# Where eight attention heads and a norm stand relative to a chunkwise delta rule, in one kernel of two transformer blocks

## The reference, cut to what matters

```
def token_mixer(h, rel_bias, w_in, conv_w, a_log, dt_bias, onorm_w, w_up_a, w_up_b, w_out):
    proj = h @ w_in
    qa, ka, va, qkv_b, z_b, b_b, a_b, gate_a, gate_b = jnp.split(proj, offs, axis=-1)
    y_a = moba_attention(heads_a(qa), heads_a(ka), heads_a(va), rel_bias)     # 8 heads of 64
    qkv_b = jax.nn.silu(causal_depthwise_conv(qkv_b, conv_w))
    q_b, k_b, v_b = (t.reshape(B, S, H_B, HD_B) for t in jnp.split(qkv_b, 3, axis=-1))
    beta = jax.nn.sigmoid(b_b)
    g = -jnp.exp(a_log) * jax.nn.softplus(a_b + dt_bias)
    o_b = gated_delta_rule(q_b, k_b, v_b, beta, g)                            # 4 heads of 128
    o_b = rms_norm(o_b, onorm_w) * jax.nn.silu(z_b.reshape(B, S, H_B, HD_B))
    y_b = o_b.reshape(B, S, W_B)
    m = jax.nn.sigmoid(gate_a) * (y_a @ w_up_a) + jax.nn.sigmoid(gate_b) * (y_b @ w_up_b)
    return m @ w_out
```

## Time and profile before

| | |
|---|---|
| runs of the kernel | 1547.35, 1551.43, 1552.74 us (median 1551.43) |
| profiled execution | 1547.66 us, span of the trace 1545.9 us |
| PE busy | 1447.2 us, 94% of the span |
| DVE, ACT busy | 763.5 us (49%), 619.6 us (40%) |
| mean granted TensorE clock | 0.949 |

### The profile page before, as it was taken

The page is one execution under the profiler, slowest core; times in us unless marked ns, Lnnn a source line. Parts: engine busy times, 40 slices in busy tenths (PEclk is TensorE's granted clock), DMA queues, the critical chain, the costliest instruction groups (busy, mean ns, idle before and its releaser), DMA issues.

```text
span 1545.9 us, 26177 instructions
## 1 busy us (share of the span) xinstructions
PE 1447.2 (94%) x10140; PEld 1233.4 (80%) x10140; DVE 763.5 (49%) x1280; ACT 619.6 (40%) x1022; POOL 10.5 (1%) x23
## 2 busy tenths in 40 slices
PE   5999999999999998899999989899878899999996
PEld 4899999899997995589999889799747856555553
DVE  4466654656545663356665456865157432221223
ACT  4445553543334552344444356533143322232222
POOL 0000020000000000000000000000000000000000
PEclk8999999999999998799999989999659899999998
DMA  7664455655556443466555454433003249999992
GB/s 311 127 187 137 137 164 177 222 174 177 177 174 218 155 150 110 145 213 221 185 190 182 160 178 150 139 108 98 26 0 123 96 184 373 366 355 371 371 367 96
DMA packets 80139, 289.65 MB, mean 187 GB/s; under 512 B 9520, under 2 KB 10544, under 8 KB 79920
## 3 DMA queue, kind: packets, MB, share of 16 engines
q1 hardware_dynamic: 77760, 280.00, 51.8%
q0 software_dynamic: 1712, 3.68, 1.6%
q10 hardware_dynamic: 576, 4.65, 0.7%
HBM read 285.14 MB, written 3.15 MB: 186 GB/s over the span
## 4 chain that ended last, share of the span: by engine, by line
PE 83%; DVE 9%; ACT 3%; DMA 2%; issue 2%; SPq 0%; ACTq 0%; DVEq 0%
PE bank L652 17%; PE bank L656 16%; PE bank L655 16%; PE bank L1184 11%; PE bank L1152 4%; DMA ring<-weights 2%; PE bank L716 2%; PE bank L793 2%; PE bank L687 1%; ACT w_hi L1255 1%; PE bank L1174 1%; PE bank L1175 1%; DVE ring_low L1641 1%; DVE hn L1656 1%; DVE sq L1976 1%
## 5 line engine op out<-in xcount | busy, mean ns | idle before, releaser
L1641 DVE TENSOR_TENSOR ring_low<-ring,w_hi 128x1024 fp32r<-128x1024 f32 x292 | 356.0, 1224 | 318.0 <-ACT w_hi L1255 315.5
L652 PE MATMUL bank<-hn_hi,w_hi 128*128 128x272 f32 (+1 forms) x1456 | 425.2, 292 | 24.2 <-DVE ring_low L1641 9.6
L656 PE MATMUL bank<-hn_hi,ring_low 128*128 128x272 f32 (+1 forms) x1456 | 418.5, 287 | 0.0
L655 PE MATMUL bank<-hn_low,w_hi 128*128 128x272 f32 (+1 forms) x1456 | 417.8, 287 | 0.0
L1255 ACT ACTIVATE w_hi<-ring 128x1024 fp32r<-128x1024 f32 x292 | 307.2, 1055 | 223.3 <-PE bank L652 181.5
L652 PEld LDWEIGHTS bank<-hn_hi,w_hi 128*128 128x128 f32 x1456 | 277.6, 191 | 31.2 <-issue 13.5
L656 PEld LDWEIGHTS bank<-hn_hi,ring_low 128*128 128x128 f32 x1456 | 278.1, 191 | 0.0
L655 PEld LDWEIGHTS bank<-hn_low,w_hi 128*128 128x128 f32 x1456 | 277.7, 191 | 0.2
L652 PE MATMUL bank<-arena_r,w_hi 128*128 128x256 f32 (+1 forms) x848 | 245.2, 289 | 12.0 <-DVE mod L1689 2.9
L656 PE MATMUL bank<-arena_r,ring_low 128*128 128x256 f32 (+1 forms) x848 | 242.8, 286 | 0.0
L655 PE MATMUL bank<-arena_r,w_hi 128*128 128x256 f32 (+1 forms) x848 | 242.3, 286 | 0.0
(11 more groups left out here) (333 smaller groups left out, 1431.5 us busy)
## 6 DMA issues: line engine op xcount, KB each, us to landing
ring<-weights SPq DMA_DIRECT2D x532, 512.0 KB, 4.4
tab<-tables ACTq DMA_DIRECT2D x1, 3129.0 KB, 12.8
skew<-arena POOLq DMA_DIRECT2D x1, 2048.0 KB, 46.4
h<-tokens ACTq DMA_DIRECT2D x2, 544.0 KB, 4.2
tab<-skew POOLq DMA_DIRECT2D x8, 128.0 KB, 3.8
out<-hn SPq DMA_DIRECT2D x8, 128.0 KB, 2.0
tab<-skew POOLq DMA_DIRECT2D x8, 64.0 KB, 3.6
vec<-vectors ACTq DMA_DIRECT2D x1, 321.5 KB, 5.1
```

The costliest lines, as they stand in the source:

```text
L652: begun = mm(dst[:, 0:cols], wh, high(k), start=k == 0, stop=False)
L655: mm(dst[:, 0:cols], wh, low(k), start=False, stop=False)
L656: last = mm(dst[:, 0:cols], wl, high(k), start=False, stop=k == K - 1)
L1641: tt_(ring_lo[:, slot, :], ring[:, slot, :], w_hi[:, n % SPLITS, :], ALU.subtract).then_inc(S("w_lo_ready"), 1)
```

## The change

Four edits, all in the second block's mixer; the mathematics is the same.

1. The attention loop is taken apart. Its scores, transposes and values get numbers among the rotating tiles (`turn`, `score`, `value`, banks 0 to 3), its buffers `p_a` and `pt_a` move into `sq`, `o_a_hi` and `o_a_lo` over and behind `q_a`. `moba(j)` on PE is: transposes of head j, scores of head j + 2, values of head j - 1. One call stands in each of nine places of the delta rule: after the gram product, after the turn of k, in levels 1 to 5 in place of the first gate tile, after `w`, and ahead of the scan. ACT and DVE get the matching pieces (`moba_exp`, `moba_turned`, `moba_store`; `moba_front`, `moba_probs`, `moba_low`).
2. The gate tiles that this displaces, and one more, move into the scan: tile 8 + 2c behind the product with the state, tile 9 + 2c behind the increment. Three of the four `z` tiles move to between gram, q by k and the turns.
3. The norms of q, k and `o_b`: the squares stand as the stationary side with one column of ones moving, so sums come out with tokens on partitions, 128 x 16 (128 x 8 for `o_b`). Root and reciprocal are taken there, and PE spreads the result back over rows by a product with the identity, two products for q and k and one for `o_b`; DVE multiplies from PSUM.
4. The weights of the two up projections are stored one after the other: all 8 half tiles of the attention (`upa`) first, with the norm of `o_b` between them, then the 8 of the delta rule (`upb`). DVE puts gate times `upa` into `m_up` and adds `upb` later.

Layout, tile order and the sums on PE:

```diff
-    out.append(narrow_units(np.concatenate([i["w_up_a_2"][0].reshape(512, DT, P), i["w_up_b_2"][0].reshape(512, DT, P)],
-                                           axis=0).reshape(D, D)))
+    out.append(narrow_units(i["w_up_a_2"][0]))
+    out.append(narrow_units(i["w_up_b_2"][0]))
...
-        tiles("z", BH, DT)
-        tiles("gates", 16, DT)
-        tiles("aa", AH, 0)
-        tiles("up", 2 * DT, 4)
...
+        z_tiles(0)
+        tiles(("score", 0), 1, 0)
+        tiles(("score", 1), 1, 0)
+        moba_tiles(0)
+        z_tiles(1)
+        z_tiles(2)
+        moba_tiles(1)
+        z_tiles(3)
+        gate_tiles(0, 2)
+        for lv in range(1, 6):
+            moba_tiles(lv + 1)
+            gate_tiles(lv + 1)
+        moba_tiles(AH - 1)
+        gate_tiles(7)
+        moba_tiles(AH)
+        gate_tiles(8, 8)
+        tiles("upa", DT, 4)
+        tiles("upb", DT, 4)
...
-            pe.wait_ge(S("exp_rows"), 1)
-            for j in range(4):
-                last = mm(bank[4 + j][:, :], ones, l2sq[:, j * 512:(j + 1) * 512], start=True, stop=True)
+            for p in range(2 * NP):
+                last = mm(bank[4][:, p:p + 1], l2sq[:, p * P:(p + 1) * P], ones[:, 0:1], start=True, stop=True)
             last.then_inc(S("l2_summed"), 1)
             wide(DT, hb, hb_lo, [(0, P), (P, SEQ)])
-            for t in range(BH):
+            pe.wait_ge(S("dec_diff"), 1)
+            pe.wait_ge(S("exp_rows"), 1)
+            pe.wait_ge(S("l2_inverted"), 1)
+            for p in range(NP, 2 * NP):
+                last = mm(bank[4 + p // 4][:, (p % 4) * P:(p % 4 + 1) * P],
+                          stats[:, 16 + p:17 + p].to_broadcast([P, P]), ident, start=True, stop=True)
+            last.then_inc(S("l2_rows"), 1)
```

The rest of PE's order:

```diff
+            def moba(j):
+
+                if j < AH:
+                    pe.wait_ge(S("moba_p"), j + 1)
+                    dst, pv = next_tile(("turn", j)), p_a[:, j % 2, :]
+                    nc.tensor.transpose(dst[:, 0:P], pv[:, 0:P], ident)
+                    nc.tensor.transpose(dst[:, P:2 * P], pv[:, P:2 * P], ident)
+                    nc.tensor.transpose(dst[:, 2 * P:3 * P], pv[:, 2 * P:3 * P], ident).then_inc(tile_done, 1)
+                if j + 2 < AH:
+                    moba_score(j + 2)
+                if j:
+                    v = j - 1
+                    if v == 0:
+                        wait_stored(pe, at["va"] + 1)
+                    dst, cols = next_tile(("value", v)), slice(v // 2 * P, (v // 2 + 1) * P)
+                    wait_stored(pe, at["turn", v])
+                    mm(dst[:, 0:SEQ], v_a[:, 0, cols], pt_a[:, v % 2, 0:SEQ], start=True, stop=False,
+                       skip_group_check=True)
+                    mm(dst[:, P:SEQ], v_a[:, 1, cols], pt_a[:, v % 2, SEQ:3 * P], start=False, stop=True,
+                       skip_group_check=True).then_inc(tile_done, 1)
+
+            hb_tile(("z", 0))
+            moba_score(0)
+            moba_score(1)
...
-            dense(DT, hb, hb_lo, SEQ)
+            moba(0)
+            hb_tile(("z", 1))
...
+            hb_tile(("z", 2))
...
+            moba(1)
+            hb_tile(("z", 3))
...
-            dense(DT, hb, hb_lo, SEQ)
-            dense(DT, hb, hb_lo, SEQ)
+            gate(0)
...
                 last.then_inc(S("mx_done"), 1)
-                dense(DT, hb, hb_lo, SEQ)
                 if lv == 0:
+                    gate(1)
                     continue
+                moba(lv + 1)
...
-                dense(DT, hb, hb_lo, SEQ)
+                gate(lv + 1)
...
-            dense(DT, hb, hb_lo, SEQ)
+            moba(AH - 1)
+            gate(7)
...
                 if c == 0:
+                    moba(AH)
...
+                gate(8 + 2 * c)
...
-            assert pos[1] == at["aa"]
-
+                gate(9 + 2 * c)
...
+            up_a()
             pe.wait_ge(S("ob_squared"), 1)
-            for j in range(2):
-                last = mm(bank[4 + j][:, :], ones, obsq[:, j * 512:(j + 1) * 512], start=True, stop=True)
+            for p in range(NP):
+                last = mm(bank[4][:, p:p + 1], obsq[:, p * P:(p + 1) * P], ones[:, 0:1], start=True, stop=True)
             last.then_inc(S("ob_summed"), 1)
...
+            up_a()
+            up_a()
+            pe.wait_ge(S("ob_inverted"), 1)
+            for p in range(NP):
+                last = mm(bank[6 + p // 4][:, (p % 4) * P:(p % 4 + 1) * P],
+                          stats[:, 8 + p:9 + p].to_broadcast([P, P]), ident, start=True, stop=True)
+            last.then_inc(S("ob_rows"), 1)
+            for t in range(3, DT):
+                up_a()
             for t in range(DT):
-                dense(4, lambda k: o_a_hi[:, k, :], lambda k: o_a_lo[:, k, :], SEQ)
                 dense(4, lambda k: o_b_hi[:, k, :], lambda k: o_b_lo[:, k, :], SEQ,
-                      (lambda k: pe.wait_ge(S("ob_split"), 1)) if t == 0 else None)
+                      (lambda k: pe.wait_ge(S("ob_split"), k // 2 + 1)) if t == 0 else None)
```

ACT:

```diff
-            for j in range(4):
-                last = fn(l2sq[:, j * 512:(j + 1) * 512], bank[4 + j][:, :], ACT.Sqrt, bias=eps_t[:, 0:1])
-            last.then_inc(S("l2_root"), 1)
+            fn(stats[:, 0:2 * NP], bank[4][:, 0:2 * NP], ACT.Sqrt, bias=eps_t[:, 0:1]).then_inc(S("l2_root"), 1)
...
+            def moba_exp(i):
+                act.wait_ge(S("moba_max"), i + 1)
+                st_i = stats[:, 64 + 8 * i:72 + 8 * i]
+                for j, (lo, hi) in enumerate([(0, P), (P, MOBA_W)]):
+                    a = p_a[:, i % 2, lo:hi]
+                    last = fn(a, a, ACT.Exp, bias=st_i[:, 2 + j:3 + j], accum_out=st_i[:, 4 + j:5 + j])
+                last.then_inc(S("moba_exp"), 1)
...
+            z(0)
+            highs(at["score", 1])
+            moba_exp(0)
+            moba_exp(1)
+            moba_turned(0)
+            z(1)
+            z(2)
+            moba_exp(2)
+            moba_turned(1)
+            moba_store(0)
+            z(3)
+            moba_exp(3)
+            gate(0)
+            gate(1)
+            for lv in range(1, 6):
+                act.wait_ge(S("mx_done"), lv + 1)
+                halves(TM, 4).then_inc(S("t_stored"), 1)
+                moba_turned(lv + 1)
+                moba_store(lv)
+                if lv + 3 < AH:
+                    moba_exp(lv + 3)
+                gate(lv + 1)
...
+                gate(9 + 2 * c)
+            highs(at["upa"])
             act.wait_ge(S("ob_summed"), 1)
+            fn(stats[:, 0:NP], bank[4][:, 0:NP], ACT.Sqrt, bias=eps_t[:, 0:1]).then_inc(S("ob_rooted"), 1)
+            highs(at["upa"] + 2)
             for j in range(2):
-                last = fn(obsq[:, j * 512:(j + 1) * 512], bank[4 + j][:, :], ACT.Sqrt, bias=eps_t[:, 0:1], scale=1.0 / BHD)
...
+                act.wait_ge(S("ob_ready"), j + 1)
+                fn(o_b_hi[:, 2 * j:2 * j + 2, :], o_b[:, 2 * j:2 * j + 2, :], ACT.Copy).then_inc(S("ob_hi_ready"), 1)
```

DVE:

```diff
-            l2_inverse(2)
-            lows_upto(before_va + 1)
-            link(l2_inverse(3))
-            tt_(flat[:, BH * SEQ:2 * BH * SEQ], flat[:, BH * SEQ:2 * BH * SEQ], l2sq[:, BH * SEQ:], ALU.mult)\
-                .then_inc(S("l2_done"), 1)
-            lows_upto(before_va + 2)
-            l2_inverse(0)
-            lows_upto(before_va + 4)
-            link(l2_inverse(1))
-            stt(flat[:, 0:BH * SEQ], flat[:, 0:BH * SEQ], BHD ** -0.5, l2sq[:, 0:BH * SEQ], ALU.mult, ALU.mult)\
-                .then_inc(S("l2_done"), 1)
...
+            link(nc.vector.reciprocal(stats[:, 16:16 + 2 * NP], stats[:, 0:2 * NP]))
+            ts_(stats[:, 16:16 + NP], stats[:, 16:16 + NP], BHD ** -0.5, None, ALU.mult).then_inc(S("l2_inverted"), 1)
+            for n in range(1, 5):
+                lows_upto(before_va + n)
+            for part in (1, 0):
+                dve.wait_ge(S("l2_rows"), 2 - part)
+                for j in range(2 * part, 2 * part + 2):
+                    a = cb[:, 2 * j:2 * j + 2, :]
+                    last = tt_(a, a, bank[4 + j][:, :].rearrange("p (a b) -> p a b", a=2), ALU.mult)
+                last.then_inc(S("l2_done"), 1)
...
+            lows(at["z", 0])
+            moba_front(0)
+            moba_front(1)
+            moba_probs(0)
...
+            dve.wait_ge(S("k_turned"), 1)
+            token_major(k_tok, 6, "bg")
+            moba_front(3)
+            moba_probs(2)
+            moba_low(0)
+            lows(at["z", 3])
...
+            dve.wait_ge(S("v_turned"), 1)
+            token_major(kd, 6, "eR")
+            token_major(v_tok, 4, "beta").then_inc(S("tok_ready"), 1)
...
                     level(lv + 1)
-                lows(at["gates"] + 3 + 2 * lv)
+                if lv + 3 < AH:
+                    moba_front(lv + 3)
+                moba_probs(lv + 2)
+                moba_low(lv)
...
-                lows(at["gates"] + 4 + 2 * lv)
...
+                lows(at["gates", 8 + 2 * c])
...
+                lows(at["gates", 9 + 2 * c])
...
```

(25 more changed lines are left out.)

264 lines of the change are left out of this document (134 added, 130 removed).

## The result

The changed kernel takes 1507.64 us (median of 4 runs, 1506.95 to 1508.16) beside 1550.61 us for the kernel before (4 runs, 1547.35 to 1552.74): ratio 0.9724, 95% interval 0.9706 to 0.9743. It is 43.0 us faster; forecast were 50.4 us and 1501.0, and the range of 1492 to 1515 holds it. The profiled execution took 1508.16 us with a span of 1506.2.

What follows compares the result with a forecast made beforehand. PE's own work was taken as the bound outside a hole at 1082 to 1237 us; stretch gains summed to 50.4 us, 1497.3 from the profiled 1547.66, or 1501.0 against the median 1551.43; range 1492 to 1515.

Steps and rivals of the forecast that it cites:

- A: End of `wide` to the first level: 34.3 us before, 29.6 after, gain 4.7.
- B: Level 0: 5.8 us, unchanged.
- D: From `u` and `w` to the scan: 7.5 us before, 8.2 after, a loss of 0.7.
- C: Levels 1 to 5: 54.0 us before, 48.3 after, gain 5.7.
- E: Scan, norm of `o_b` and attention: 77.4 us before, 36.9 after, gain 40.5.
- F: Up projections to the last operand of `wout`: 31.05 us before, 30.8 after, gain 0.2.
- (b): Clock falls again inside the new order: 1504 to 1511 us, 1538 with the whole scan at 0.50; chance 0.20.
- (a): Over all stretches, the forecast sum holds within its small terms: 1493 to 1507 us; chance 0.60.
- (c): The heads' ACT and DVE chains show in the levels: 1510 to 1519 us, milder form 1506; chance 0.13.
- (d): Slower than before, PE at 0.50 through the interleaved part: 1650 us with all of it; chance 0.02.
- (e): Better: DVE stays ahead in the up projections and early waits before the levels vanish: 1487 to 1493 us; chance 0.05.

Runs made afterwards that it cites:

- early high part: Changed kernel with ScalarE making the high part of each `w_up_b` weight unit one tile earlier, ahead of its copy of `m_up`: 1506.47 us.
- second series: The changed kernel run once more without any edit, beside the other follow-up runs: median 1511.74 us of 6 runs.
- spread sums: Changed kernel with the 8-column and one-column matmuls placed among wide ones instead of in rows: 1507.51 us.

## Why the prediction was right, and where its terms were off

**A, B and D** came within 0.4 us, with the 1.46 us wait at the first transposes that was counted as 1.4. The smaller wait of 0.7 for `tok_ready` isn't there.

**C, 1.1 us too low.** A level takes 10.36 us, not 10.1; PE is busy for 41.48 of 41.50, so it isn't a wait. I had taken a head's 1.7 us from single rows; in the level it costs 2.0 (1043.46 to 1045.49), and the tile that it displaces 2.9 and not 2.84. The room of ScalarE and VectorE was as counted: the heads' pieces cost nothing, and two more table switches per level cost nothing either.

**E, 2.3 us too low.** Two terms failed, about one half each. The tiles did hold the clock at 1.00, but "24.5 us at clock 0.50, so 12.3 at full clock" is too low for the smallest matmuls. Their pairs, before and after:

```profile
1096.16 0.69 PE L1063 MATMUL bank<-arena 128*128 128x64 f32 x2 [0.78 <-DVE arena L2057]
1096.78 0.69 PE L1064 MATMUL bank<-arena 64*128 64x64 f32 x2
```

```profile
1100.81 0.43 PE L1157 MATMUL bank<-arena 64*128 64x64 f32 x2
1101.17 0.43 PE L1156 MATMUL bank<-arena 128*128 128x64 f32 x2
```

They start 0.62 us apart at 0.50 and 0.36 at 1.00, so the output of a chunk takes 2.7 us and not half of 4.81; the products with the state and the increments, 1.0 each, did halve. The scan's own work is 15.3 us where I had 14.2. The other term is "eight gate tiles 22.7": in the scan they take 23.9, 2.94 to 3.04 each and not 2.84, a price that came from tiles behind tiles, while each of these stands between products.

**F, 2.6 us too low.** The step is "1.8 us per `upb` tile". Its own operations are as counted, 3.45 to 3.5 per two tiles; left out was a wait of 1.10 us in every second tile for the high part of the weights, which ScalarE makes only behind the copy of `m_up`, which waits for VectorE's addition. The early high part shows it: F is 3.1 us shorter with it, 30.3 (1133.2 to 1163.5) against the forecast 30.8, and 1.2 us of clock come back behind it.

**Where the 45 us come from** is shown by taking parts away: the heads in the gaps are worth 38.6 to 41.5, the tiles in the scan 16.8. Taken singly they come to more than 45, as parts do that lie over each other's waits: with the heads gone, the levels wait too (5.9 us), and the one-piece attention is idle and slow. The norms of q and k alone are worth about 1.8 us in one profile and lose them to the clock there. The norm of `o_b` with tokens on partitions was not run alone, so its share is not shown.

**The number, and rival (b).** With A to F as measured the forecast is 5.3 us higher, 1506.3. The range of rival (a), 1493 to 1507, misses the measured 1507.64 by a little, and the 1504 to 1511 of rival (b) holds it; but the profile that belongs to the result has none of (b)'s falls between the norms and the end of the up projections, so the number is (a)'s sum with C, E and F too low, and that it also suits (b) is chance. From execution to execution (b) does come and go: the second series has two falls there, worth 4.6 us, and its median is 4.1 us higher (1511.74). The forecast's 1501 had neither these nor C, E and F. The full clock of the levels before was a weak argument against falls behind idle time, as PE was busy there for 60.8 of 61.8 us.

**Rivals (c) and (d)**: no wait for `moba_probs` but the first, no level longer for lack of ScalarE, and in the result's profile no stretch at 0.50 in the interleaved part; one of 3.4 us stands in the scan with spread sums. (d)'s 1650 should have been 1660, 1501 and 159. (e) had DVE staying ahead in F; it didn't, and with the early high part it still ends F, at 3.45 us per two tiles against PE's 2.84.

What stays open: why the clock falls behind the one-column sums in seven profiles and not in two others, and behind the 1.46 us wait at the first transposes in five of nine. The experiments show what precedes a fall, not what decides it.

## What to carry to other kernels

A chain between three engines costs only its own TensorE time in the gaps of another chain, and all its waits in one piece: the same eight heads, with the same instructions, added 9 to 12 us here and 50 there. Look for idle time that comes with a clock of 0.50, as it pays twice. When work is moved to another clock, don't halve small matmuls; and for the engine that will end a stretch, write down its list together with the list of the engine that feeds it, since one copy in the wrong order cost 1.1 us in every second tile. Price a tile where it will stand: 2.84 us behind another tile was 2.94 to 3.04 between products. A difference of 4 us needs several executions of both kernels, or a stretch in the profile.

## What the runs showed of the hardware

The granted clock fell with PE busy without a gap: 3.2 us into a row of 8-column matmuls (914.1, ahead of it 31 instructions in 3.20 us of 3.20), and behind a row of 32 one-column matmuls in seven profiles, among them the second of the changed kernel and that of the norms alone, but not in the first profile of the same program. Spread among wide ones, the same narrow matmuls ran at 1.00 in both profiles. Behind the wait of 2.8 us at the end of the up projections it fell in seven profiles of seven, and with a wait of 0.88 in its place in none of two. Pairs of float32 matmuls with 64 columns start 0.62 us apart at 0.50 and 0.36 at 1.00. The two levels in these stretches are 2.4 GHz (1.00) and 1.2 (0.50). A table switch of ScalarE is 1.30 us in all, with the load 0.02 us behind one activation and the next activation 0.01 to 0.02 us behind the load.
